# Two heads per step in the attention pipeline of a two-model forward pass

## The reference

```python
# causal self attention (16 heads of 64), bias by distance; the latent layer also masks unselected keys
l = jnp.einsum('hqd,hkd->hqk', q, k) * scale + bias          # NEG where the key is not allowed
p = jax.nn.softmax(l, axis=-1)
o = jnp.einsum('hqk,hkd->hqd', p, v)
# differential attention (8 heads, value width 128): two score maps per head of 64 features each
p = softmax(l1) - lam * softmax(l2);  o = p @ v
# cross attention (4 heads of 256, 256 memory rows), no bias
```

## Time and profile before

| | us |
|---|---|
| median of three runs | 3164.3 |
| profiled execution, from its first to its last instruction | 3169.5 |
| block attention | 122.3 to 180.5: 58.2 |
| latent attention | 497.0 to 558.2: 61.2 |
| first cross attention | 1310.8 to 1328.8: 18.0 |
| differential attention | 1663.7 to 1697.6: 33.9 |
| second cross attention | 1851.7 to 1870.5: 18.8 |

### The profile page before, as it was taken

The page is one execution under the profiler, slowest core; times in us unless marked ns, Lnnn a source line. Parts: engine busy times, 40 slices in busy tenths (PEclk is TensorE's granted clock), DMA queues, the critical chain, the costliest instruction groups (busy, mean ns, idle before and its releaser), DMA issues. The chain is left out here.

```text
span 3169.5 us, 38932 instructions
## 1 busy us (share of the span) xinstructions
PE 2772.2 (87%) x14405; PEld 2307.3 (73%) x14406; DVE 1912.7 (60%) x2351; ACT 1496.5 (47%) x1824; POOL 88.0 (3%) x96
## 2 busy tenths in 40 slices
PE   4989987898766868999898888999999899898998
PEld 3769864697746647689875867877787678787877
DVE  2445516455559954354436446977454788797978
ACT  2444423444221024344334435866444667686866
POOL 0000002000002300000010000000000000000000
PEclk8889985899868889899998987999999999999999
DMA  9325430355100034245441424978555798797976
GB/s 251 109 95 186 157 107 1 126 191 182 37 7 1 1 133 146 79 158 189 147 133 64 137 73 177 376 288 304 164 185 182 248 338 319 280 379 283 375 275 230
DMA packets 333367, 563.51 MB, mean 178 GB/s; under 512 B 21977, under 2 KB 126616, under 8 KB 332984
## 3 DMA queue, kind: packets, MB, share of 16 engines
q1 hardware_dynamic: 333112, 560.22, 51.8%
HBM read 555.99 MB, written 4.19 MB: 177 GB/s over the span
## 5 line engine op out<-in xcount | busy, mean ns | idle before, releaser
L1057 DVE TENSOR_TENSOR weights_split<-ring,weights_split 128x1024 fp32r<-128x1024 f32 x676 | 818.9, 1224 | 250.3 <-ACT weights_split L1052 206.3
L1101 PE MATMUL ps<-weights_split,expert_split 128*128 128x512 f32 x3864 | 908.0, 395 | 37.4 <-issue 34.6
L1052 ACT ACTIVATE weights_split<-ring 128x1024 fp32r<-128x1024 f32 x676 | 714.8, 1061 | 341.0 <-PE ps L1101 334.7
L1101 PEld LDWEIGHTS ps<-weights_split,expert_split 128*128 128x128 f32 x3864 | 729.9, 190 | 193.3 <-issue 39.2
L289 DVE TENSOR_TENSOR weights_split<-ring,weights_split 128x2048 fp32r<-128x2048 f32 x182 | 413.5, 2273 | 536.4 <-ACT weights_split L280 536.4
L280 ACT ACTIVATE weights_split<-ring 128x2048 fp32r<-128x2048 f32 x182 | 345.4, 1899 | 502.1 <-PE ps L365 501.7
L365 PE MATMUL ps<-normed_split,weights_split 128*128 128x256 f32 (+1 forms) x4320 | 533.8, 285 | 45.2 <-PEq L342 43.6
L365 PEld LDWEIGHTS ps<-normed_split,weights_split 128*128 128x128 f32 (+1 forms) x4320 | 530.8, 193 | 51.6 <-issue 46.7
L365 PE MATMUL ps<-weights_split,hidden_split 128*128 128x512 f32 x1032 | 242.6, 391 | 4.3 <-DVE hidden_split L522 4.3
L365 PEld LDWEIGHTS ps<-weights_split,hidden_split 128*128 128x128 f32 x1032 | 190.8, 188 | 44.0 <-DVE hidden_split L522 6.0
L365 PE MATMUL ps<-weights_split,normed_split 128*128 128x512 f32 (+1 forms) x816 | 194.7, 399 | 26.0 <-DVE weights_split L289 16.1
(11 more groups left out here) (337 smaller groups left out, 2313.5 us busy)
## 6 DMA issues: line engine op xcount, KB each, us to landing
ring<-moe_w_gate SPq DMA_DIRECT2D x112, 1024.0 KB, 6.5
ring<-moe_w_up SPq DMA_DIRECT2D x112, 1024.0 KB, 6.6
ring<-moe_w_down SPq DMA_DIRECT2D x112, 1024.0 KB, 6.6
ring<-mlp_w_up SPq DMA_DIRECT2D x32, 1024.0 KB, 5.4
ring<-mlp_w_down SPq DMA_DIRECT2D x32, 1024.0 KB, 4.9
ring<-xa_w_kv SPq DMA_DIRECT2D x16, 1024.0 KB, 5.2
ring<-moba_w_qkv SPq DMA_DIRECT2D x12, 1024.0 KB, 11.3
ring<-da_w_qkv SPq DMA_DIRECT2D x12, 1024.0 KB, 5.1
```

What stands on the lines that cost most here:

```text
L1052: nc.scalar.activation(split_piece(p, 0), ring_piece(p), ACT.Copy).then_inc(high.sem, 1)
L1057: nc.vector.tensor_tensor(split_piece(p, 1), ring_piece(p), split_piece(p, 0).bitcast(F32), ALU.subtract)\
L1101: last = nc.tensor.matmul(ps[:, banks[half][tt], :], stationary(s, k, tt), split_piece(p, i)[:, kk * NW:(kk + 1) * NW], start=(opens and n ...
```

## The change

All engine programs of `attention` are rewritten to work in groups.

- `G` units are done per step: 2 in the 16-head and in the differential attention, 1 in cross attention. `F` heads are transposed per step: 2 in the 16-head attentions, 1 elsewhere.
- Score products are issued tile by tile, alternating between the two units, whose operands lie in different halves of the partitions (rows of the PE array). They go to four banks instead of two.
- Value products of two heads alternate too, and their outputs lie in different halves of the partitions of one bank (columns of the array). Two banks take them instead of four.
- The transposes of a pair go to one bank per head (4 and 5) instead of two alternating ones, so that PE waits for the copies of the pair just before (`copied.at(2 * t)`); before, it waited for the copy of two heads before.
- The biased scores go straight to `p_sb` (six buffers), the exponential is taken in place, and `s_sb` is gone. The wait of DVE for the exponential two units back becomes one for the transposes six units back. `pT` has four buffers.
- The negation and the reciprocal are done once per step on four columns instead of twice on two. The wait for the score bank and the wait for exponentials are per step.
- GpSimd waits for a new semaphore `attn_scored`, counted per unit, as `attn_negmax` now counts steps.

```diff
--- before.py
+++ after.py
-    scores, negmax, expd, probs, flipped, copied, outs, kept = (
+    G = 2 if pair or comps == 2 else 1
+    F = 2 if pair else 1
+    steps = units // G
+    NP, NT = (6, 4) if causal else (4, 2)
+    scores, scored, negmax, expd, probs, flipped, copied, outs, kept = (
         core.sig(f"attn_{n}") for n in
-        ("scores", "negmax", "expd", "probs", "flipped", "copied", "outs", "kept"))
-    s_sb = core.a(scratch, 2 * 512).rearrange("p (b n) -> p b n", b=2)
-    p_sb = core.a(scratch + 1024, 4 * 512).rearrange("p (b n) -> p b n", b=4)
-    pT = core.a(scratch + 3072, 2 * 512).rearrange("p (b n) -> p b n", b=2)
+        ("scores", "scored", "negmax", "expd", "probs", "flipped", "copied", "outs", "kept"))
+    p_sb = core.a(scratch, NP * W).rearrange("p (b n) -> p b n", b=NP)
+    pT = core.a(scratch + NP * W, NT * W).rearrange("p (b n) -> p b n", b=NT)
     nmx = core.a(scratch + 4096, 2 * units)
     sums = core.a(scratch + 4096 + 2 * units, 2 * units)
     rs = core.a(scratch + 4096 + 4 * units, 2 * units)
+    score_bank = lambda u: u % (2 * G)
+    flip_bank = lambda t, f: 4 + (f if F == 2 else t % 2)
     def pe(e):
+        for s in range(steps + 3):
+            if s < steps:
+                if s >= 2:
+                    e.wait_ge(*(negmax.at(s - 1) if bias else expd.at(G * (s - 1))))
+                for tt in range(TT):
+                    lo, n = spans[tt]
+                    for g in range(G):
+                        u = s * G + g
+                        ql, kl = q_rows(u, tt), k_rows(u, n)
+                        for i, (q, k) in enumerate(zip(ql, kl)):
+                            last = nc.tensor.matmul(core.ps[:, score_bank(u), lo:lo + n], q, k,
+                                                    start=(i == 0), stop=(i == len(ql) - 1))
+                last.then_inc(*scores.up())
+            if 2 <= s <= steps + 1:
+                t = s - 2
+                e.wait_ge(*probs.at(G * (t + 1)))
+                if F == 2 and t >= 1:
+                    e.wait_ge(*copied.at(2 * t))
+                if F == 1 and t >= 2:
+                    e.wait_ge(*copied.at(t - 1))
+                for f in range(F):
...
+                t = s - 3
+                e.wait_ge(*copied.at(F * (t + 1)))
+                if t >= 2:
+                    e.wait_ge(*kept.at(t - 1))
...
-                        if kt == 0 or not causal:
-                            cols, src = (d * T, T), pT[:, h % 2, kt * T:(kt + 1) * T]
-                        else:
-                            cols, src = (d * T + P, P), pT[:, h % 2, T:T + P]
-                                                start=(kt == 0), stop=(kt == 1))
+                        for f in range(F):
+                            b = (F * t + f) % NT
+                            if kt == 0 or not causal:
+                                cols, src = (d * T, T), pT[:, b, kt * T:(kt + 1) * T]
+                            else:
+                                cols, src = (d * T + P, P), pT[:, b, T:T + P]
+                            m0 = DH * f
+                            last = nc.tensor.matmul(core.ps[m0:m0 + m, 6 + t % 2, cols[0]:cols[0] + cols[1]],
+                                                    vN[:, kt, v_cols(F * t + f) + d * P:v_cols(F * t + f) + d * P + m],
+                                                    src, start=(kt == 0), stop=(kt == 1))
                 last.then_inc(*outs.up())
...
-                    e.wait_ge(*negmax.at(u + 1))
-                    if u >= 4:
-                        e.wait_ge(*flipped.at((u - 4) // comps + 1))
+        for s in range(steps + 3):
+            if s < steps:
+                e.wait_ge(*negmax.at(s + 1))
+                for u in range(s * G, s * G + G):
+                    if not bias and u >= NP:
+                        e.wait_ge(*flipped.at((u - NP) * F // G + 1))
                     for tt in range(TT):
...
+            if 2 <= s <= steps + 1:
+                t = s - 2
+                for f in range(F):
+                    e.wait_ge(*flipped.at(F * t + f + 1))
+                    if t >= NT // F:
+                        e.wait_ge(*outs.at(t - NT // F + 1))
+                    nc.scalar.activation(pT[:, (F * t + f) % NT, 0:W], core.ps[:, flip_bank(t, f), 0:W], ACT.Copy)\
+                        .then_inc(*copied.up())
             if s >= 3:
-                h = s - 3
-                if not pair or h % 2 == 1:
-                    o = h // 2 if pair else h
-                    e.wait_ge(*outs.at(h + 1))
-                    nc.scalar.activation(oT[:, o * nd:(o + 1) * nd, :].rearrange("p a t -> p (a t)"),
-                                         core.ps[:, 4 + o % 4, 0:nd * T], ACT.Copy).then_inc(*kept.up())
+                t = s - 3
+                e.wait_ge(*outs.at(t + 1))
+                nc.scalar.activation(oT[:, t * nd:(t + 1) * nd, :].rearrange("p a t -> p (a t)"),
+                                     core.ps[:, 6 + t % 2, 0:nd * T], ACT.Copy).then_inc(*kept.up())
...
                 if bias:
-                    b = bias(e, u)
-                    if u >= 2:
-                        e.wait_ge(*expd.at(u - 1))
+                    for u in us:
+                        b = bias(e, u)
+                        if u >= NP:
+                            e.wait_ge(*flipped.at((u - NP) * F // G + 1))
+                        for tt in range(TT):
+                            lo, n = spans[tt]
+                            last = nc.vector.tensor_tensor_reduce(
+                                out=p_sb[:, u % NP, lo:lo + n], in0=core.ps[:, score_bank(u), lo:lo + n], in1=b[tt],
+                                scale=1.0, scalar=-3e38, op0=ALU.add, op1=ALU.max,
+                                accum_out=rs[:, 2 * u + tt:2 * u + tt + 1])
+                        last.then_inc(*scored.up())
+                    e.wait_ge(*scored.at(G * (s + 1)))
+                    nc.vector.tensor_scalar(nmx[:, cells], rs[:, cells], -1.0, None, ALU.mult).then_inc(*negmax.up())
...
+                e.wait_ge(*expd.at(G * (t + 1)))
+                cells = slice(2 * t * G, 2 * (t + 1) * G)
+                core.link(e, "dve", nc.vector.reciprocal(rs[:, cells], sums[:, cells]))
+                for w in range(t * G, t * G + G):
+                    second = comps == 2 and w % 2 == 1
+                    if second:
+                        core.link(e, "dve", nc.vector.tensor_scalar(rs[:, 2 * w:2 * w + 2], rs[:, 2 * w:2 * w + 2],
+                                                                    lam, None, ALU.mult))
+                        e.wait_ge(*probs.at(w))
...
+                    last.then_inc(*probs.up())
@@ -2298,7 +2313,7 @@
         def pool(e):
             for u in range(H):
                 if u >= 2:
-                    e.wait_ge(*sig("attn_negmax").at(u - 1))
+                    e.wait_ge(*sig("attn_scored").at(u - 1))
                 nc.gpsimd.tensor_tensor(tmp[:, u % 2, 0:P], toep[:, u, P:T], sel[:, 0:P], ALU.add)
                 nc.gpsimd.tensor_tensor(tmp[:, u % 2, P:CAUS], toep[:, u, :], sel[:, P:CAUS], ALU.add)\
```

More of the change, by code:

```diff
@@ L699, in attention @@
     rs = core.a(scratch + 4096 + 4 * units, 2 * units)
+    score_bank = lambda u: u % (2 * G)
+    flip_bank = lambda t, f: 4 + (f if F == 2 else t % 2)
     def pe(e):
[L702 to L705, removed]
-                    if u >= 2:
-                        e.wait_ge(*(negmax if bias else expd).at(u - 1))
+        for s in range(steps + 3):
[19 more added lines that the diff above has]
+                for f in range(F):
+                    u = t * G + (f if pair else G - 1)
@@ L709, in pe @@
                     for tt in range(TT):
                         lo, n = spans[tt]
[L711 to L728, removed]
@@ L729, in pe @@
-            if s >= 3:
-                h = s - 3
-                e.wait_ge(*copied.at(h + 1))
-                o = h // 2 if pair else h
-                if o >= 4 and (not pair or h % 2 == 0):
-                    e.wait_ge(*kept.at(o - 3))
+                        for kt in range(n // P):
+                            at = (kt * T + tt * P) if (kt == 0 or not causal) else T
+                            last = nc.tensor.transpose(core.ps[:, flip_bank(t, f), at:at + P],
+                                                       p_sb[:, u % NP, lo + kt * P:lo + (kt + 1) * P], core.c("ident"))
@@ L777, in dve @@
-    def dve(e):
-        for u in range(units + 1):
-            if u < units:
-                e.wait_ge(*scores.at(u + 1))
-                if bias:
-                    b = bias(e, u)
-                    if u >= 2:
-                        e.wait_ge(*expd.at(u - 1))
+            if 2 <= s <= steps + 1:
[6 more added lines that the diff above has]
+                        .then_inc(*copied.up())
@@ L797, in dve @@
[L797 to L815 removed]
+                        p = p_sb[:, w % NP, lo:lo + n]
@@ L817, in attention @@
+                        r = rs[:, 2 * w + tt:2 * w + tt + 1]
```

(6 more changed lines are left out.)

62 lines of the change are left out of this document (16 added, 46 removed).

## The result

The kernel changed takes 3113.99 us (median of 4 runs, 3112.64 to 3115.28) against 3162.93 us of the kernel before in the same comparison (4 runs, 3160.57 to 3168.37): ratio 0.984, interval 0.9827 to 0.9854, 48.9 us less. The forecast was 3115 us.

A forecast was written before the change was run, and what follows sets the result against it. PE at the low clock was taken as the bound, 3.88 us a head. Block 24.4, latent 25.0 and differential 3.0 make 52.4, less 3.4 for low periods: 49 off 3164.3 gives 3115.3 us, range 3107 to 3128.

The forecast's parts named there:

- PE's durations: PE, per pair: scores 1.6, transposes 1.5, values 1.5 us, 4.6 at the low clock; 2.6 at the high one.
- The chain: Scores through bias, exponentials, copies, transposes and values over two steps: 8.8 us at low clock, 6.8 (3.4 a pair) at high.
- Block attention: Block attention stage: 19.7 us less at the low clock, 24.4 less with the high clock from the third transposes.
- Latent attention: Latent attention stage: 21.3 us less at the low clock; 25.0 less at the high one, where DVE's 3.6 a pair bounds.
- Differential attention: Differential attention stage: fewer negations and reciprocals, scores side by side; 3 us less, range 0 to 6.
- The clock: 16-head stages: expected to rise as paired scores use all rows; 52.4 us less if high, 44.0 if low.
- 3.4 us off for low steps: Both 16-head stages: one or two of five periods still low, about 1.1 us each, taking 52.4 to 49 us.
- a later stage that grows: Sign of being wrong: the attention stages shrink and a later one grows; all other stages should keep their length.
- the low clock: Rival: the clock stays low in both 16-head stages, 44 us less, 3120 us; chance 25%.
- the columns: Rival: column halves do not overlap, values cost 2.94 us instead of 1.5, 23 less gain, 3143 us; chance 8%.
- the bank: Rival: the single transposed bank bites, 5.2 to 6 us a pair, 10 to 20 less gain, about 3130 us; chance 10%.
- the closed chain: Rival: the chain closes every step, 8.8 us a pair instead of 7.76, 17 us slower, 3181 us; chance 3%.

The follow-up runs named there:

- before_full_rows: Kernel before, with block and latent attention scores contracted over all 128 partitions instead of 64: 3128.92 us, ratio 0.9876 to the kernel before.
- both_lower: Kernel changed, with both units' scores on the lower 64 rows and both heads' values on the lower 64 output partitions: 3132.73 us, ratio 0.9885.
- cols_lower: Kernel changed, with both heads' value products on the lower 64 output partitions, one head after the other: 3121.28 us, ratio 0.9856.
- the three kernels that shorten it: Kernel changed with negation per unit in 16-head attentions, transposes waiting per head, or both: 3115.73, 3113.76 and 3110.93 us.
- second profile: Unaltered kernels profiled again: kernel before 3166.97 us in its one run; kernel changed 3111.34 us, ratio 0.9832.
- early_both: Kernel changed, with negation per unit in the 16-head attentions and transposes waiting per head: 3110.93 us, ratio 0.9809.
- early_in_block: Kernel changed, with transposes waiting per head in both 16-head stages and negation per unit in block attention alone: 3108.34 us, ratio 0.9816.
- the second comparison: Kernel changed, unaltered, timed again beside the kernel before: 3111.34 us, ratio 0.9832, 55 us less.

## Why the prediction was right, and where it was lucky

**What bounds the kernel: right, but half told.** PE at the low clock set 3.88 us a head. I took the clock as a second term beside the halving of PE's work. It is the first: before_full_rows gets 39.8 us with no instruction fewer, by way of the clock, and both_lower 35 with no overlap. The kernel changed gets 49 to 55. The parts overlap and can't be added.

**PE's durations: right.** Scores 1.65 and 0.93 (forecast 1.66 and 0.93), transposes 1.54 and 0.85 (1.5 and 0.87 to the next), values 0.87 busy (0.85 to the next). The reading of the first 8 records in the earlier trace rows and of the column halves in the earlier trace rows held, the latter at 256 columns too, shown by cols_lower. The rule of the Trainium skill (TensorE: Matmul & The Clock Gate, Part 3) that a weight load passes a running matmul only in another row group did not hold the column halves apart here: 0.87 us against 1.51. It speaks of weight loads and not of the matmuls, so I had read more into it than it states.

**The chain: right.** 6.8 us over two steps forecast, 6.75 measured; PE 2.6 of 3.4. That it, and not ACT, is the bound, the three kernels that shorten it show: 6.19, 6.41 and 5.86 us for two steps.

**Block attention: 33.8 forecast with the high clock, 30.4 and 32.1 measured.** It lies under the 34 to 38.5 us that I had named as a sign. First transposes after 5.5 us forecast and 5.6 measured. Two sizes were off. The clock rose before the third transposes in the first profile (3.3 us behind the second instead of 4.6). And the last transposes came 1.6 us behind those before (150.65 to 152.22), not 3.4: at the end no scores and no exponentials are left in the chain. For the low clock I had taken the scores off, for the high one nothing.

**Latent attention: 36.1 forecast, 35.3 and 35.4 measured.** This too is just under the 36 to 40 that I had named. The stretch of DVE beside GpSimd is real, with four scalings at 1.57 us and a negation of 0.66 against 0.17; the negation I had not seen coming. Two of the steps at the high clock took 3.48 and 3.75 us, around the 3.6 forecast; the last took 1.6, as in block attention.

**Differential attention: 3 forecast, 3.3 and 4.3 measured** (33.9 to 30.6, and 29.5 in the second profile). **Cross attention: nothing forecast;** 18.0 and 18.8 us became 18.1 and 18.0, and 17.6 and 18.7 in the second profile, while the second profile of before has 17.6 and 18.1.

**The clock: the reason was partly wrong.** I wrote that it stayed low while every second matmul used half of the rows; by the earlier trace rows it was 4 of 11 records, 1.58 of 3.88 us. Full rows do raise it (before_full_rows), yet with half-row scores it rises too, in a kernel with the transposes and values of two heads together (both_lower). What of that order raises it stays open, and whether transposes count towards it too. And I took 3.4 us off for low steps behind the third transposes in both stages; in the first profile there was none, in the second part of one in block attention (137.79 to 142.10, 4.31 us). The low clock fell on the steps before instead.

**Where the sum was lucky.** The attention stages give back 56 to 58 us in the profiles, not 49. For a profiled execution I had forecast 3120.5 us, and it took 3110.8: there the 9.7 us show. (I also compared a span with a time in the step from one to the other; the profiled execution of before was 7 us above the median of my three runs, not 5.2.) Against the attention stages, the projection behind block attention is 1.6 us longer in both profiles of after (25.2 us before, 26.8 after, from barrier to barrier): the clock falls in it from 156.9 to 160.3, which it didn't before. I had named a later stage that grows as a sign of being wrong. It is a small one, and in early_both and early_in_block the projection lasts 25.2 again. The rest between 49 and these 56 to 58 lies in the scatter: medians of before were 3162.9 to 3168.7 us, and the first comparison had the lowest. Against the other three medians of before, 3113.99 is 52 to 55 us less, and the second comparison gave 55. The forecast of 49 lies 3 to 6 us under these, and its hit to 1 us is more than it had earned. Of the rivals, the low clock, the columns, the bank and the closed chain did not come. Why the unprofiled runs gain 49 to 55 and the profiles 56 to 58 us in attention is settled only to these few us.

## What to carry to other kernels

Read the granted clock of a stage before counting instructions in it: where TensorE is busy all the time at 0.5, the first question is what would raise the clock, and grouping like matmuls or using all rows may be worth more than doing less. The fp32 matmuls here, in different row halves or column halves, ran side by side in both orders of issue, so put the two heads of a pair into one stretch and let the waits, not the loop order, be the concern. When PE becomes quick, walk the chain through the other engines over two steps, and look for what the last steps no longer contain.

## What the runs showed of the hardware

- With the same records and columns, scores over 128 rows instead of 64 kept the clock at 1.00 in block attention, where it had been 0.56 (34.9 against 58.2 us).
- With half-row scores, and no two matmuls in different halves, the rewritten order (two heads' transposes and values together, 4.2 us) had a mean clock of 0.82 in the same stage and 0.65 in the latent one. Which part of the rewrite does it was not tested.
- Eight value records in two column halves took 0.87 us, in one half 1.51; eight score records at the low clock 1.65 in two row halves, 2.93 in one.
- A vector operation on 128x4 elements took 0.66 us beside a GpSimd operation on two tensors, 0.17 without; a reduction over PSUM beside it kept its 0.42.
- Executions of one kernel (that of before) on a single core differed by up to 9.5 us (3161.79 to 3171.33 in one comparison). Between its two profiles, 4.4 us apart, one stage differs by 2.9 us at clocks of 0.89 and 0.95.
